# First head pair by eight half products, and the mixer norm's weight multiplied into rows before they are turned

## The reference

```python
u = rmsnorm(h, norm_mix[layer])          # x * rsqrt(mean(x*x) + eps) * norm_mix, per token
proj = u @ w_in[layer]
qa, ka, va, qd, kd, vd, z, beta_raw, a_raw, gate_raw = jnp.split(proj, split_at, axis=-1)
# 12 attention heads of width 128 (3 groups of dilation 1, 4, 16), 8 gated DeltaNet heads
beta = jax.nn.sigmoid(beta_raw)
g = -jnp.exp(a_log) * jax.nn.softplus(a_raw + dt_bias)
```

## Time and profile before

| what | value |
|---|---|
| median of three runs | 2330.04 us (2328.87 to 2330.37) |
| the profiled execution's own time | 2330.01 us |
| its span, first to last instruction | 2328.3 us |
| PE matmul busy | 2205.2 us, 95% of the span |
| PE weight load busy | 1829.3 us, 79% |
| DVE, ACT, POOL busy | 1079.8, 937.3, 694.2 us (46%, 40%, 30%) |

### The profile page before, as it was taken

The page is one execution under the profiler, slowest core; times in us unless marked ns, Lnnn a source line. Parts: engine busy times, 40 slices in busy tenths (PEclk is TensorE's granted clock), DMA queues, the critical chain, the costliest instruction groups (busy, mean ns, idle before and its releaser), DMA issues.

```text
span 2328.3 us, 30636 instructions
## 1 busy us (share of the span) xinstructions
PE 2205.2 (95%) x11016; PEld 1829.3 (79%) x11016; DVE 1079.8 (46%) x1470; ACT 937.3 (40%) x1597; POOL 694.2 (30%) x536
## 2 busy tenths in 40 slices
PE   5599999999999999999999999997899999999997
PEld 4488788787887888888888887885688888878886
DVE  6622331323237666656656543423755555550153
ACT  5344444444435545555654641122433333330012
POOL 6487565656522111111111124321000000043330
PEclk8799999999999999999999999998899999999999
DMA  5122212222132202211221343331122222261221
GB/s 111 29 60 68 74 55 65 87 69 74 55 94 80 64 18 72 63 36 45 63 61 29 127 150 114 93 87 45 55 82 81 81 81 81 81 223 48 89 56 73
DMA packets 249953, 175.64 MB, mean 75 GB/s; under 512 B 41272, under 2 KB 225784, under 8 KB 249872
## 3 DMA queue, kind: packets, MB, share of 16 engines
q1 hardware_dynamic: 219808, 136.46, 20.0%
q10 hardware_dynamic: 30064, 38.10, 5.2%
HBM read 143.36 MB, written 31.18 MB: 75 GB/s over the span
## 4 chain that ended last, share of the span: by engine, by line
PE 87%; DVE 5%; ACT 2%; issue 2%; DMA 1%; DVEq 1%; ACTq 1%; POOL 0%; SPq 0%; POOLq 0%
PE bank L213 20%; PE bank L2070 18%; PE bank L1013 16%; PE bank L2298 10%; PE bank L1218 5%; PE bank L1468 2%; PE bank L1451 2%; PE bank L701 1%; PE bank L1458 1%; DVE own_sum_t L488 1%; PE bank L712 1%; PE bank L1505 1%; PE bank L1500 1%; PE bank L1501 1%; PE bank L1487 1%
## 5 line engine op out<-in xcount | busy, mean ns | idle before, releaser
L213 PE MATMUL bank<-u_hi,w_hi 128*128 128x512 f32 x704 | 311.5, 442 | 6.1 <-ACT z_next L1685 4.8
L199 POOL CAST w_hi<-raw 128x1024 fp32r<-128x1024 f32 (+1 forms) x60 | 62.0, 1034 | 726.4 <-PE bank L213 511.6
L213 PE MATMUL bank<-u_hi,w_lo 128*128 128x512 f32 x704 | 277.0, 393 | 0.0
L213 PE MATMUL bank<-u_lo,w_hi 128*128 128x512 f32 x704 | 276.4, 393 | 0.0
L2258 POOL CAST dn_hi<-dn_raw 128x896 fp32r<-128x896 f32 (+1 forms) x24 | 26.0, 1085 | 590.6 <-DMA dn_raw<-in_w_down 482.3
L213 PEld LDWEIGHTS bank<-u_hi,w_lo 128*128 128x128 f32 x704 | 132.5, 188 | 29.3
L201 POOL TENSOR_TENSOR w_lo<-raw,w_hi 128x1024 fp32r<-128x1024 f32 (+1 forms) x60 | 149.0, 2483 | 8.6
L213 PEld LDWEIGHTS bank<-u_hi,w_hi 128*128 128x128 f32 x704 | 134.0, 190 | 22.2 <-ACT z_next L1685 5.3
L946 POOL TENSOR_TENSOR q_lo_s<-q_sum_s,q_hi_s 128x512 fp32r<-128x512 f32 x96 | 125.5, 1312 | 79.9 <-ACT q_hi_s L985 74.2
L213 PEld LDWEIGHTS bank<-u_lo,w_hi 128*128 128x128 f32 x704 | 134.2, 191 | 14.9 <-issue 1.9
L2298 PE MATMUL bank<-v_hi,dn_lo 128*128 128x512 f32 x352 | 136.9, 389 | 0.0
(11 more groups left out here) (367 smaller groups left out, 5605.2 us busy)
## 6 DMA issues: line engine op xcount, KB each, us to landing
raw<-in_w_in SPq DMA_DIRECT2D x36, 512.0 KB, 3.9
raw_first<-in_w_in SPq DMA_DIRECT2D x24, 512.0 KB, 3.9
raw_second<-in_w_in SPq DMA_DIRECT2D x24, 512.0 KB, 4.6
row<-scr_rows ACTq DMA_DIRECT2D x24, 512.0 KB, 4.7
raw_gate<-in_w_gate SPq DMA_DIRECT2D x22, 512.0 KB, 4.0
raw_up<-in_w_up SPq DMA_DIRECT2D x22, 512.0 KB, 3.9
scr_v<-gate_out SPq DMA_DIRECT2D x44, 256.0 KB, 2.6
v_in<-scr_v SPq DMA_DIRECT2D x11, 1024.0 KB, 8.5
```

The source lines that it names most:

```text
L199: nc.gpsimd.tensor_copy(hi[:, 0:kt, :], raw[slot][:, 0:kt, :])
L213: last = nc.tensor.matmul(bank[dst][:, :], wpart[slot][wp][:, k, :], rhs[ap][:, k, half * HALF:(half + 1) * HALF], start=k == 0 and (wp, a ...
```

## The change

- norm_mix is loaded as one row, spread over the partitions by two matmuls with a row of ones, copied to norm_mix_all, and multiplied in by scale: a scalar_tensor_tensor with rstd and norm_mix_all in place of the tensor_scalar. What is turned is then already u.
- Of a turned chunk ScalarE takes the first half (cast to u_hi, copy to u32), VectorE copies the second half to u32 and ScalarE casts it from there. The low part of the first half is GpSimd's, that of the second half VectorE's (low(c), one chunk late).
- All 48 matmuls of beta_decay come after the last transpose.
- Pair 0 (first_pair_pe) is computed as four outputs of 8 slices x 3 matmuls each (96 matmuls, not 84) from u_hi, u_lo and the weight quarters a, b, c, d alone. The j loop of the first (slot, group) has 60 steps, of which 32 are these.
- The sums t1 to t4 are needed first in pair 1; they are made in the order t1, t3, t2, t4, and their casts and low parts are spread over the steps of pairs 0 and 1.
- The decay steps are spread anew: the reciprocal (L607) is replaced by an Ln and an Exp on ScalarE, one subtraction by another instruction form, and the eight transposes come in the last product of pair 1.
- ScalarE loads the table with Ln ahead of the chunks (a preload), and ahead of roots(1).

```diff
+            sp.dma_start(norm_mix_row[:, :], norm_mix).then_inc(params, 16)
...
-                for q in range(2):
-                    pool.wait_ge(x_high, 2 * c + q + 1)
-                    g.tensor_tensor(act_in[1][:, 4 * q:4 * q + 4, c * P:(c + 1) * P],
-                                    u32[:, c, 4 * q:4 * q + 4, :],
-                                    act_in[0][:, 4 * q:4 * q + 4, c * P:(c + 1) * P].bitcast(F32),
-                                    ALU.subtract).then_inc(x_low, 1)
+                pool.wait_ge(x_weighted, 2 * (c + 1))
+                g.tensor_tensor(act_in[1][:, 0:4, c * P:(c + 1) * P], u32[:, c, 0:4, :],
+                                act_in[0][:, 0:4, c * P:(c + 1) * P].bitcast(F32), ALU.subtract).then_inc(x_low, 1)
...
+            nc.scalar.preload_act_table_set("natural_log")
             for c in range(KT):
-                for q in range(2):
-                    act.wait_ge(x_weighted, 2 * c + q + 1)
-                    nc.scalar.activation(act_in[0][:, 4 * q:4 * q + 4, c * P:(c + 1) * P],
-                                         u32[:, c, 4 * q:4 * q + 4, :], ACT.Copy).then_inc(x_high, 1)
+                act.wait_ge(x_turned, 2 * c + 1)
+                nc.scalar.activation(act_in[0][:, 0:4, c * P:(c + 1) * P], turned_rows(c, 0), ACT.Copy).then_inc(x_high, 1)
+                nc.scalar.activation(u32[:, c, 0:4, :], turned_rows(c, 0), ACT.Copy).then_inc(x_weighted, 2)
+                act.wait_ge(qp["sums"], c + 1)
+                nc.scalar.activation(act_in[0][:, 4:8, c * P:(c + 1) * P], u32[:, c, 4:8, :], ACT.Copy).then_inc(x_high, 1)
...
-            part_high(act, 0, "a")
-            part_high(act, 0, "c")
+            for name in ("a", "c", "b", "d"):
+                part_high(act, 0, name)
             operand_cast(act, "t1")
...
+            operand_cast(act, "t3")
...
+            act.wait_ge(qp["sums"], KT + OPERAND[o])
+            if o == "t2":
+                act.wait_ge(qp["done"], 7)
+            elif o == "t4":
+                act.wait_ge(qp["low"], 3)
...
-                v.tensor_scalar(xn[:, c % 2, :], x_rows[:, c, :], rstd[:, c:c + 1], None,
-                                ALU.mult).then_inc(x_scaled, 1)
+                v.scalar_tensor_tensor(xn[:, c % 2, :], x_rows[:, c, :], rstd[:, c:c + 1], norm_mix_all[:, :],
+                                       ALU.mult, ALU.mult).then_inc(x_scaled, 1)
+
+            dve.wait_ge(params, 17)
+            for q in range(2):
+                v.tensor_copy(norm_mix_all[:, q * HALF:(q + 1) * HALF], bank[Y0 + q][:, :])
...
+            def low(c):
+                dve.wait_ge(x_high, 2 * c + 2)
+                v.tensor_tensor(act_in[1][:, 4:8, c * P:(c + 1) * P], u32[:, c, 4:8, :],
+                                act_in[0][:, 4:8, c * P:(c + 1) * P].bitcast(F32), ALU.subtract).then_inc(ba_split, 1)
+
...
-                for q in range(2):
-                    dve.wait_ge(x_turned, 2 * c + q + 1)
-                    v.tensor_tensor(u32[:, c, 4 * q:4 * q + 4, :],
-                                    bank[XB[c % 2][q]][:, :].rearrange("p (f t) -> p f t", t=P),
-                                    norm_mix_c[:, 4 * q:4 * q + 4].unsqueeze(2).broadcast_to([P, 4, P]),
-                                    ALU.mult).then_inc(x_weighted, 1)
+                dve.wait_ge(x_turned, 2 * c + 2)
+                v.tensor_copy(u32[:, c, 4:8, :], turned_rows(c, 1)).then_inc(qp["sums"], 1)
+                if c:
+                    low(c - 1)
+            low(KT - 1)
+            dve.wait_ge(x_weighted, 2 * KT)
...
+            for o, first, second in (("t1", u_part(0, 1), u_part(0, 0)), ("t3", u_part(1, 1), u_part(0, 1)),
+                                     ("t2", u_part(1, 1), by_chunk("t1")),
+                                     ("t4", u_part(1, 0), by_chunk("t2"))):
...
+            pe.wait_ge(params, 16)
+            pe.wait_ge(consts, 1)
+            for q in range(2):
+                last = nc.tensor.matmul(bank[Y0 + q][:, :], ones[0:1, :], norm_mix_row[:, q * HALF:(q + 1) * HALF],
+                                        start=True, stop=True)
+            last.then_inc(params, 1)
...
-                        pe.wait_ge(x_weighted, 2 * (c - 2) + q + 1)
+                        if q == 0:
+                            pe.wait_ge(x_weighted, 2 * (c - 1))
+                        else:
+                            pe.wait_ge(qp["sums"], c - 1)
...
-                if c >= KT // 2:
-
-                    if c == KT // 2:
-                        pe.wait_ge(ba_split, 1)
-                        pe.wait_ge(x_low, KT)
-                    for k in (2 * c - KT, 2 * c - KT + 1):
-                        beta_decay(0, k)
-            pe.wait_ge(x_low, 2 * KT)
-            for k in range(KT):
-                beta_decay(1, k)
+            for half in range(2):
+                pe.wait_ge(x_low, KT // 2 * (half + 1))
+                pe.wait_ge(ba_split, 1 + KT // 2 * (half + 1))
+                for k in range(KT):
+                    beta_decay(half, k)
...
+            elif j == 16:
+                part_high(act, 1, "s1")
+                part_high(act, 1, "s2")
+            elif j == 24:
...
-                f(row_t[1][a8, :], row_t[1][a8, :], ACT.Ln, bias=1.0).then_inc(ba_act, 1)
-            elif j == 30:
+                f(row_t[1][a8, :], row_t[1][a8, :], ACT.Ln, bias=1.0)
+                f(row_t[1][b8, :], row_t[1][b8, :], ACT.Ln, bias=1.0).then_inc(ba_act, 1)
+            elif j == 37:
+                act.wait_ge(ba_act, 4)
+                act.wait_ge(ba_vec, 2)
+                f(rows[a8, :], row_t[1][b8, :], ACT.Exp, scale=-1.0).then_inc(ba_act, 1)
+                operand_cast(act, "t4")
...
             if j == 8:
+                operand_low(dve, "t1")
+            elif j == 10:
+                dve.wait_ge(kept, 16)
+                dve.wait_ge(x_low, KT)
+                dve.wait_ge(ba_act, 3)
+                dve.wait_ge(rate_loaded, 32)
+                v.tensor_scalar(row_t[0][a8, :], row_t[0][a8, :], rate[a8, 2:3], None, ALU.add)
...
+                dve.drain()
+                v.scalar_tensor_tensor(row_t[2][a8, :], row_t[0][a8, :], -1.0, row_t[0][a8, :], ALU.mult,
+                                       ALU.min).then_inc(ba_vec, 1)
                 operand_low(dve, "t3")
-            elif j == 9:
...
+            elif j == 24:
+                dve.wait_ge(ba_act, 4)
+                v.scalar_tensor_tensor(row_t[1][a8, :], row_t[0][a8, :], 0.0, row_t[1][a8, :], ALU.max, ALU.add)
+                dve.drain()
+                v.tensor_scalar(row_t[2][b8, :], row_t[1][a8, :], rate[a8, 1:2], -1.0, ALU.mult,
+                                ALU.mult).then_inc(ba_vec, 1)
+                dve.drain()
+                v.tensor_tensor_scan(rows[b8, :], reset[:, :], row_t[2][b8, :], 0.0, ALU.mult, ALU.add)
+            elif j == 32:
+                operand_low(dve, "t2")
...
+            elif j == 42:
                 operand_low(dve, "t4")
...
+        FIRST_PART_AT = {"a": 1, "c": 2, "b": 3, "d": 7}
+        FIRST_FREE = {"a": 4, "c": 4, "s4": 7, "d": 7}
+        FIRST_OUT = (("a", "c", 0), ("a", "c", 1), ("b", "d", 0), ("b", "d", 1))
...
+        def first_pair_pe(pe, j):
+
+            o, k = j // 8, j % 8
+            low_part, high_part, half = FIRST_OUT[o]
+            name = low_part if k < 4 else high_part
+            if k % 4 == 0:
+                pe.wait_ge(qp["part"], FIRST_PART_AT[name])
+                if k == 0:
+                    wait(pe, qp["copied"], o - 1)
+            for wp, ap in PASSES:
+                last = nc.tensor.matmul(bank[D1 - half][:, :], (q_hi, q_lo)[wp][name][:, k % 4, :],
+                                        act_in[ap][:, k, half * HALF:(half + 1) * HALF],
+                                        start=k == 0 and (wp, ap) == PASSES[0], stop=k == 7 and (wp, ap) == PASSES[-1])
+            if k == 7:
+                last.then_inc(qp["done"], 1 if o == 3 else 2)
+
+        def first_pair_act(act, j):
+
+            if j % 8 != 7:
+                return
+            o = j // 8
+            half = o % 2
+            act.wait_ge(qp["done"], (2, 4, 6, 7)[o])
+            if o == 0:
+                act.wait_ge(qp["sums"], KT + 4)
+                act.wait_ge(x_low, KT)
+            nc.scalar.activation(qk_t[0][o // 2][:, half * HALF:(half + 1) * HALF], bank[D1 - half][:, :], ACT.Copy,
+                                 scale=1.0 if o // 2 else float(P) ** -0.5).then_inc(qp["copied"], 1)
+            if o == 1:
+                part_high(act, 1, "a")
+                part_high(act, 1, "c")
+            elif o == 2:
+                part_high(act, 1, "s3")
+            elif o == 3:
+                operand_cast(act, "t2")
+                part_high(act, 1, "s4")
 
...
-                if q == 0 and o[0] == "t":
+                if q == 1 and o[0] == "t":
                     pe.wait_ge(qp["low"], OPERAND[o])
-                if m in (0, 3, 6):
+                if q == 1 and m == 0:
```

(58 more changed lines are left out.)

147 lines of the change are left out of this document (67 added, 80 removed).

## The result

The changed kernel takes 2307.22 us (median of 4 runs, 2302.60 to 2310.91) against 2330.20 (2328.87 to 2331.56, 4 runs) on the same chip: ratio 0.990, 95% interval 0.9881 to 0.9919, so 23 us less where 29.7 were forecast. The profiled execution took 2307.56 us with a span of 2305.8, against 2330.01 and 2328.3.

The account below looks back on a forecast made before the run. PE's own stream was taken to bound the kernel, with 55 us without PE work up front. Terms -1.2 - 32.7 + 4.2 = -29.7 put pair 2 at 97.5 and the time at 2300.3 us; forecast 2294 to 2307, range 2292 to 2311.

Parts of the forecast that it names:

- Pair 0: First pair's 96 matmuls run without waits at full clock: 21.8 us instead of 54.5, a gain of 32.7 us.
- Chunk stage: Work before the first pair: 3.0 us a chunk, first pair starting at 51.1, 1.2 us earlier; bounds 47 and 57.
- Pair 1: Second pair loses 4.2 us: 2.1 waiting for t2, 0.7 slow matmuls, 1.4 at its end; bounds -4, +5.
- The chain itself: ScalarE's Ln, VectorE's decay, then t2's low part, ready at 80.4; PE wants it at 78.3 and waits 2.1 us.
- The end of the pair: Second pair's eight transposes: PE waits 1.4 us behind ScalarE's three DMA issues and s3 cast; bounds 0 and 3.
- From pair 2 on: Everything after the third pair's start stays fixed relative to it, 2201.1 us, so the whole gain reaches the end.
- a sign of being wrong: One listed sign against the forecast: a later stage that gives back over 3 us.
- Rival A: The t operands are late again: 9 us more waiting and 1.5 of slow matmuls, 2311 us; chance 0.17.
- B: Chunk stage shortens through rarer turns and early warm PE, first pair starting at 47: 2293 us; chance 0.12.
- C: Little reaches the end: stages behind 127 us take back 10 to 20 us, giving 2310 to 2320; chance 0.04.
- D: Slower: PE stays at 1.2 GHz through beta_decay and the first two pairs, 42 us more, 2342; chance 0.04.
- E: No change, if the head of the kernel were hidden by something else; chance 0.02.

Follow-up runs that it names:

- five orders: Changed kernel with t2's low part before the scan, side masks one pair later, row stores behind per_token copies, s3 and s4 casts behind the last copies: 2299.92 us.

## Why the prediction came out as it did

**The time** (2300.3 forecast, 2307.22 measured) lies inside the range of 2292 to 2311, a little above the inner range of 2294 to 2307. The main step was right; that the total came as near has some luck in it, for the chunk stage gave 1.9 us more than forecast for a reason not named, against 7.1 us lost in pair 1 and 2.0 given back later. By steps:

- **Pair 0** (forecast 21.8 us, a gain of 32.7): 70.96 - 49.20 = 21.76, no wait, full clock; the gain is 54.46 - 21.76 = 32.7. Right in size, and all the waits of the earlier trace rows are gone. The wait for t2 goes because this pair no longer reads it. The two others were for take-outs in lists that the change also orders anew; no run keeps the seven products of pair 0 with the new lists, so what the lists alone would have given is not known.
- **Chunk stage** (forecast 1.2 sooner): 3.1 sooner, and for a reason I did not name. A chunk's period was forecast at 3.0 us and is 2.88 (scales at 30.82 and 33.70). The last transposes end at 37.0, not 38.5. But with the old stage in its place they end at 36.2 and pair 0 starts at 48.45. What had cost time before was that half of beta_decay stood between the transposes and waited there for GpSimd's low parts (3.38 us at 30.81), which held up the transposes behind it; moving it gives 3.8 us alone.
- **Pair 1** (forecast a loss of 4.2): 31.74 - 20.40 = 11.3 lost. A window over just this pair has PE busy 20.40 of 20.40 us before and 23.78 of 31.74 now: 8.0 us idle (forecast 3.5) and 3.4 more for the same matmuls at the low clock behind the waits (forecast 0.7). This is the step that failed in size: the loss is outside the upper bound of its own term too (5 us over 4.2). Its cause was named rightly, t2's low part late behind the decay: forecast 2.1 us with bounds 0 and 6, measured 4.5. Most of the difference is that PE comes sooner: pair 0 began 1.9 us earlier than forecast, so PE wants t2 at 76.56 and not at 78.3. The chain itself starts 0.9 early (the second Ln at 71.46 ends at 72.5, where 73.4 was forecast) and ends 0.6 late, at 81.00: VectorE's tensor_scalar and scan took 1.63 and 3.25 us instead of 1.0 and 2.3. Alone they take 0.74 and 2.28, and each began with some 1.1 us of a GpSimd instruction left to run; the forecast had such turns in its bounds and none in its sum. (Its sum for this chain is also 0.4 above the terms it is made of: they give 80.0, not 80.4.) The end of the pair was forecast at 1.4 us with bounds 0 and 3. It has waits of 0.3 + 1.5 + 1.5 = 3.3, and the slow matmuls and transposes behind them. The forecast saw s3's cast and the DMA issues in front of the first copies, but not s4's cast in front of the last ones. That these orders make most of the excess is shown: changed one by one they move the waits about, changed together they give 26.40 instead of 31.74 us, near the 24.6 of the forecast.
- **From pair 2 on** (forecast: nothing is given back): 24.5 becomes 22.5, and in the second execution of the same kernel 25.0 becomes 20.0, more than the 3 us that the forecast named as a sign of being wrong. The step from pair 14 to 15 takes 29.6 us, 27.2 before. ScalarE waits there for the store of the gate tile's other half:

```profile
394.82 0.60 ACT L1135 ACTIVATE gate_part<-bank 128x512 f32<-128x512 f32 x1 [3.42 <-DMA scr_gate<-gate_part]
395.45 0.33 ACTq L1146 DMA_DIRECT2D scr_gate<-gate_part  x1
...
395.56 0.47 PE L1084 MATMUL bank<-u_hi,q_hi_c 128*128 128x512 f32 x1 [1.98 <-ACT gate_part L1135]
```

The longest such wait of ScalarE was 2.0 before, is 3.4 here, and the step is 30.2 in the second execution of the same kernel, 26.7 with the old chunks, 27.0 with the side masks later and with five orders. The traces of all versions agree: where this one wait is 3.3 to 3.5 us (six of them) the step takes 28.6 to 30.2, where it is 1.7 to 1.8 it takes 26.7 to 27.3. So the wait and the loss go together. What makes the store land late is open: that it is where the pairs' starts fall against the loads that share the DMA queues is a guess, and neither a second gate tile nor a shorter store was run. Nor does this wait make all of the scatter. The second execution lost 1.6 us more in pair 2, at the lower clock; and the profiled execution with t2 ahead of the scan, the slowest of its five (2313.63 us), lost 4 us behind the start of the last pair.

Rival A was right in part and too dear: it put 9 us of waiting more and 1.5 of slow matmuls there; the waits of pair 1 are 7.8 us where the forecast had 3.5, and the loss is 7.1 larger in all. The operand t2 was late within the forecast's bounds; the other half of the waits is for the copies of the decay, not for operands. B was wrong in its ground: fewer turns on GpSimd do nothing. C is seen in small, 2 us given back and not 10 to 20. D and E did not occur: the clock rose 3.1 us after beta_decay's start at 36.65 and stayed up to the end of pair 0.

The rule quoted from the Trainium skill (SBUF — State Buffer, "Who interferes with whom"), whole instructions blocking each other, agrees with the scale of 2.28 beside GpSimd: 1.28 alone, and GpSimd's subtraction had 1.20 us left when it began. It agrees with low(c) too. By the rule the later one waits for what is left of the other, not for all of it: when low(c) began at 32.62, GpSimd's subtraction (from 31.58, 1.64 long) had 0.60 left, and 0.69 + 0.60 = 1.29 is near the 1.16 measured.

## What to carry to other kernels

Before pricing an edit that rearranges many instructions, list what it moves on the engine that sets the end, here PE, and price each move by itself: a step between two other steps that waits for a slow engine was worth more than all the sharing of work around it. An engine that comes somewhere sooner waits there if what it needs does not come sooner as well, as PE did for t2. When waits follow each other on one path, a single reordering only hands its gain to the next wait; write down for each engine everything in front of the instruction waited for, to the last one, and change the orders together. An instruction that waits for another engine, here a cast for a later pair, must stand behind all short ones that somebody waits for at once.

## What the runs showed of the hardware

With GpSimd and VectorE both reading SBUF, either can be the one that is stretched, and narrow instructions as much as wide ones. On GpSimd a subtraction of 128x512 that takes 1.28 us alone took 5.50, and a 128x128 select 3.42 instead of 0.29, while VectorE ran the scan and low parts of 128x2048:

```profile
75.39 1.28 POOL L961 TENSOR_TENSOR q_lo_s<-q_sum_s,q_hi_s 128x512 fp32r<-128x512 f32 x1 [0.47 <-ACT q_hi_s L1016]
76.64 5.50 POOL L961 TENSOR_TENSOR q_lo_d<-raw_second,q_hi_d 128x512 fp32r<-128x512 f32 x1
82.11 0.74 POOL L384 TENSOR_SCALAR_AFFINE_SELECT neg_upper<-neg_upper 128x128 f32<-128x128 f32 x1
82.91 3.42 POOL L386 TENSOR_SCALAR_AFFINE_SELECT strict_up<-ones 128x128 f32<-128x128 f32 x1
```

The scan alone, in the kernel before:

```profile
96.52 2.28 DVE L612 TENSOR_TENSOR_SCAN rows<-reset,row_t 8x1024 f32<-8x1024 f32 x1
```

The sizes come out to within 0.2 us if the instruction that begins second waits for the rest of the one that runs. The scan over only 8 partitions takes 2.28 us alone; it took 3.25 where GpSimd's subtraction (from 75.39) had 1.10 left. A tensor_scalar of the same shape took 1.63 and not 0.74 with 1.09 left, a copy 1.74 and not 0.68 with 1.19 left. GpSimd's 5.50 began under the scan, and VectorE's low part followed the scan at once, up to 81.00: 4.36 of waiting and 1.28 of its own make 5.64. So in a chain of such instructions the price of a turn is neither nothing nor a fixed amount: it is what the other engine has left at that moment, and instructions that follow each other without a pause on one engine can hold the other for all of them. The forecast's sum had no turn in the chain for t2, and the trace has two.
